# Front in one schedule: input in pieces, latent units by chunk, mask as contraction rows, attentions interleaved, output projection in halves

## The reference, cut to what matters

```python
n = rms_norm(h, attn_norm)
z = n @ w_in                     # gq, gk, gv, g_low, g_r, c_q, c_kv, k_r
# gated linear attention, 4 heads, chunks of 64
log_a = log_sigmoid(g_low @ gla_gate_w2 + gla_gate_b) / 16
o_g = rms_norm(gla_chunked(gq * 64 ** -0.5, gk, gv, log_a), gla_out_norm) * silu(g_r)
# latent attention, 8 heads of 96 (64 plain, 32 rotated)
q_m = rms_norm(c_q, mla_q_norm) @ mla_w_uq
k_nope, v_m = rms_norm(c_kv, mla_kv_norm) @ mla_w_ukv
q_m, k_m = rope(rms_norm(q_m, qk_norm_q)), rope(rms_norm([k_nope, k_r], qk_norm_k))
o_m = softmax(q_m @ k_m.T / sqrt(96), masked by chunk of 64) @ v_m
h = h + concat(o_g, o_m) @ w_out
h = h + square(relu(rms_norm(h, mlp_norm) @ w_mlp_up)) @ w_mlp_down    # and so on, not touched
```

## Time and profile before

| | |
|---|---|
| median of three timed runs | 1779.61 us (1776.09 to 1781.24) |
| profiled execution | 1769.77 us, span 1768.0 us |
| mean granted TensorE clock | 0.981 |
| busy | TensorE 97%, VectorE 55%, ScalarE 34%, GpSimd 8% |
| chain that ended last | TensorE 86%, VectorE 9%, ScalarE 2%, DMA 2% |
| loads of a 1 MB unit | 125, 4.8 us to landing |

### The profile page before, as it was taken

How to read it: one execution, slowest core, us unless ns; L and a number is a source line. 1 busy time by engine, 2 the same in 40 slices (tenths; PEclk the granted TensorE clock), 3 DMA queues, 4 the chain that set the end, 5 groups by cost and what they waited for, 6 DMA issues and landing times.

```text
span 1768.0 us, 19415 instructions
## 1 busy us (share of the span) xinstructions
PE 1713.6 (97%) x8226; PEld 1375.6 (78%) x8226; DVE 970.9 (55%) x1407; ACT 598.4 (34%) x832; POOL 149.8 (8%) x107
## 2 busy tenths in 40 slices
PE   5898999999999999999999999999999999999999
PEld 3776667878888888887888888887776888888887
DVE  5576654544434346675755645754647567456453
ACT  2243432432323133342322322344556433222211
POOL 2151000200000000240000000041100200000000
PEclk9997979999999999999999999999999999999999
DMA  4211000333333242221232222322212123222221
GB/s 173 96 66 54 1 1 1 108 90 140 90 116 102 104 122 97 72 72 63 104 119 96 95 97 77 128 79 101 76 60 95 48 95 113 102 96 95 96 77 66
DMA packets 27016, 154.00 MB, mean 87 GB/s; under 512 B 4657, under 2 KB 5825, under 8 KB 10929
## 3 DMA queue, kind: packets, MB, share of 16 engines
q1 hardware_dynamic: 24048, 147.62, 23.4%
q0 software_dynamic: 2592, 4.41, 1.7%
q10 hardware_dynamic: 288, 0.73, 0.1%
HBM read 148.01 MB, written 4.72 MB: 86 GB/s over the span
## 4 chain that ended last, share of the span: by engine, by line
PE 86%; DVE 9%; ACT 2%; DMA 2%; issue 1%; POOL 1%; SPq 0%; DVEq 0%; ACTq 0%; POOLq 0%
PE bank L519 22%; PE bank L521 22%; PE bank L520 22%; PE bank L525 3%; PE bank L527 3%; PE bank L526 3%; DVE WL L1513 2%; DMA RAW<-in_W 2%; PE bank L688 1%; PE bank L1087 1%; PE bank L1109 1%; PE bank L1096 1%; PE bank L715 1%; ACT WH L1153 1%; PE bank L689 1%; PE bank L728 1%
## 5 line engine op out<-in xcount | busy, mean ns | idle before, releaser
L519 PE MATMUL bank<-AH,WH 128*128 128x512 f32 (+1 forms) x1184 | 469.4, 396 | 21.1 <-DVE AL L1537 16.2
L521 PE MATMUL bank<-AH,WL 128*128 128x512 f32 (+1 forms) x1184 | 464.8, 393 | 0.0
L520 PE MATMUL bank<-AL,WH 128*128 128x512 f32 (+1 forms) x1184 | 464.3, 392 | 0.0
L1513 DVE TENSOR_TENSOR WL<-RAW,WH 128x2048 fp32r<-128x2048 f32 (+2 forms) x137 | 307.4, 2246 | 214.8 <-ACT WH L1153 214.8
L1153 ACT ACTIVATE WH<-RAW 128x2048 fp32r<-128x2048 f32 (+2 forms) x137 | 254.0, 1857 | 304.1 <-PE bank L521 258.8
L519 PEld LDWEIGHTS bank<-AH,WH 128*128 128x128 f32 (+1 forms) x1184 | 223.7, 189 | 74.8 <-issue 14.5
L520 PEld LDWEIGHTS bank<-AL,WH 128*128 128x128 f32 (+1 forms) x1184 | 223.9, 189 | 48.0 <-issue 2.1
L521 PEld LDWEIGHTS bank<-AH,WL 128*128 128x128 f32 (+1 forms) x1184 | 223.5, 189 | 48.2 <-issue 1.4
L519 PE MATMUL bank<-HH,WH 128*128 128x512 f32 x608 | 239.6, 394 | 0.0
L521 PE MATMUL bank<-HH,WL 128*128 128x512 f32 x608 | 238.4, 392 | 0.0
L520 PE MATMUL bank<-HL,WH 128*128 128x512 f32 x608 | 236.0, 388 | 0.0
(11 more groups left out here) (273 smaller groups left out, 1807.7 us busy)
## 6 DMA issues: line engine op xcount, KB each, us to landing
RAW<-in_W SPq DMA_DIRECT2D x125, 1024.0 KB, 4.8
RAW<-in_W SPq DMA_DIRECT2D x9, 768.0 KB, 4.3
ev_scratch<-ev POOLq DMA_DIRECT2D x4, 640.0 KB, 29.0
X<-in_XT SPq DMA_DIRECT2D x4, 512.0 KB, 10.5
Gb<-ev_scratch SPq DMA_DIRECT2D x16, 128.0 KB, 2.9
out<-X SPq DMA_DIRECT2D x8, 256.0 KB, 2.0
Gb<-ev_scratch SPq DMA_DIRECT2D x16, 112.0 KB, 2.6
RAW<-in_W SPq DMA_DIRECT2D x2, 512.0 KB, 6.2
```

What stands on the lines that cost most here:

```text
L519: e.matmul(o, a, h, start=first, stop=False)
L520: e.matmul(o, a, l, start=False, stop=False)
L521: return e.matmul(o, c, h, start=False, stop=last)
L1513: e.tensor_tensor(k.WL[u % NW][:, 0:n], k.RAW[u % NR][:, 0:n], k.WH[u % NW][:, 0:n].bitcast(F), SUB).then_inc(*WLO.mark(u))
```

## The change

- Input: eight pieces of one tile, on two queues; ScalarE makes `AH`, VectorE only `AL` and the additions of the squares, GpSimd none. The constants are loaded after the input.
- Latent units by chunk: `small` and `ckv` become one unit of 192 columns (`lkv`); it and `cq` are multiplied channel tile by channel tile as `AL` comes. `norm_spread` follows both. `gq` goes between the column sums. Six banks rotate instead of four.
- Heads: `qm` and `km` hold heads outside and 100 instead of 96 columns; columns 96 to 99 hold, per block of 128 tokens, a one (query, first chunk) or -1e30 (key, second chunk), so the score product masks itself. Gains go into the copy of the transposed head (plain part) and into the rotation's tables; the query's root goes into the exponential's scale, one root of 32 columns per side instead of four of 8.
- Steps: one head transpose per step, ahead of use, all copied by ScalarE, into four query and four key buffers; the maximum is taken by an operation that also copies the scores out; the weights are scaled by VectorE and turned by a transpose.
- Output projection: units by half of the channels. `attended` takes the attention's half for all eight output tiles, between the linear attention's last stages; the other half follows as two more units. `X` gets two additions per tile. `AT` lies in the `RAW` buffer that the first MLP unit loads into, so that load waits for the last low part `ol`. The MLP's norm takes tiles 4 to 7 first.

```diff
-        for x in range(4):
-            a, l = split_view(k, wu[x // 2], 8)
...
+    for c in range(4):
+        low_and_values(c)
+    for c in range(4):
+        low_queries(c)
+    for c in range(4, 8):
+        low_and_values(c)
+        low_queries(c)
...
-                e.matmul(bank[b][:, 0:n], k.qT[hh][0:MQ, q * P:(q + 1) * P], k.kT[hh][0:MQ, 0:n], start=True, stop=True)
-                e.matmul(bank[b][:, n - P:n], cst[0:1, C_MA:C_MA + P], cst[0:1, C_MB:C_MB + P], start=False, stop=True,
-                         skip_group_check=True).then_inc(*MM.mark("s1", i, hh))
+                e.matmul(bank[hh][:, 0:n], k.qT[y][0:MK, q * P:(q + 1) * P], k.kT[y][0:MK, 0:n], start=True, stop=True).then_inc(
+                    *MM.mark("s1", i, hh))
...
-                    t = e.matmul(bank[4 + hh][:, c * P:(c + 1) * P], pb[2 * (u % 3) + hh][:, c * P:(c + 1) * P], dg[:, x, :],
-                                 start=True, stop=True, skip_group_check=True)
+                    t = e.transpose(bank[4 + hh][:, c * P:(c + 1) * P], pb[2 * (u % 3) + hh][:, c * P:(c + 1) * P], ident)
...
+        if i < 3 * NT:
+            head(q % 2, 2 * p + 2 + q // 2, 2)
...
+    attended(0)
+    attended(1)
+    outputs(0)
+    attended(2)
+    outputs(1)
+    attended(3)
+    out_sums(0)
+    out_sums(1)
+    attended(4)
+    out_sums(2)
+    out_sums(3)
+    attended(5)
+    spread_out(0)
+    attended(6)
+    spread_out(1)
+    attended(7)
+    spread_out(2)
+    spread_out(3)
...
# scalar_program
+    fill(4)
+    split(6)
     for q in range(NT):
-        fill(1)
         w.wait_ge(MM("ukv", q, 1), POOL("rq3"))
         e.activation(k.vm[:, q, :], bank[k.where["ukv", q, 1]][:, :], AF.Copy, scale=k.rq3[:, 4 + q:5 + q]).then_inc(*ACT.mark("vm", q))
...
# sync_program
+        if u == UNIT["up", 0]:
+            w.wait_ge(DVE("ol", 3))
```

More of the change, by code:

```diff
@@ L480, in fill_order @@
 def fill_order():
[L482 to L492, removed]
+    out = [("squares", 0, q) for q in range(NT)]
+    out += [("root", 0, 0), ("angles", 0, 0), ("tables", 0, 0), ("turn1", 0, 0), ("turn2", 0, 0)]
+    out += [("squares", 1, q) for q in range(NT)]
+    out += [("root", 1, 0), ("tables", 1, 0), ("turn1", 1, 0), ("turn2", 1, 0)]
+    return out + [("norm", 1, q) for q in range(NT)]
 def mla_steps():
@@ L673, in tensor_program, with head @@
     ptb = k.t2s + sq
+    def head(x, g, b):
+        w.wait_ge(DVE("norm1", 3) if x else DVE("rope", 0), POOL("seen"), *free[b])
+        for c in range(NT):
+            t = e.transpose(bank[b][0:MK, c * P:(c + 1) * P], (k.qm, k.km)[x][:, g, c, :], ident)
+        t.then_inc(*in_bank(b, "head", x, g))
+        free[b] = [ACT("head", x, g)]
+    for n, (x, g) in enumerate(((0, 0), (0, 1), (1, 0), (1, 1))):
+        head(x, g, (2, 4, 5, 6)[n])
     for i, p, q in mla_steps():
-        if p < MH // 2:
+        if i < 4 * NT:
@@ L862, in low_of @@
+    MM.also("unit", u)
+    u = UNIT["wout", 3]
+    a, l = split_view(k, u, 4)
+    w.wait_ge(WLO(u))
+    for x in range(4):
+        cols = slice(x * P, x * P + P)
+        b = (6, 7, 4, 5)[x]
+        w.wait_ge(*free[b])
+        for c in range(4):
+            t = triple(bank[b][:, :], a[:, c, cols], l[:, c, cols], AH[:, c, :], AL[:, c, :], c == 0, c == 3)
+        t.then_inc(*in_bank(b, "res", 16, x))
+        free[b] = [DVE("x", 16, x)]
+    MM.also("unit", u)
+    ring[0] = 0
     def low_of(n):
@@ L1558, in vector_program, with scaled_query @@
             *DVE.mark("cl", i))
+    def scaled_query(i):
+        w.wait_ge(MM("gq", i))
+        e.scalar_tensor_tensor(k.gq[:, i, :], bank[where["gq", i]][:, :], GK ** -0.5, rb[:, :], MUL, MUL).then_inc(*DVE.mark("gq", i))
+    low_rank(0)
+    low_rank(1)
+    low_rank(2)
+    split(3)
+    scaled_query(0)
+    w.wait_ge(MM("small"))
+    e.tensor_tensor(k.low[:, :], bank[where["small",]][0:64, :], rb[0:64, :], MUL).then_inc(*DVE.mark("low"))
     w.wait_ge(MM("csum", 2))
@@ L1663, in vector_program @@
             fill(2)
-    for half in range(2):
-        split(11 + half)
-        for q in range(NT):
-            fill(1)
-            if half:
-                w.wait_ge(MM("gv", 1, q))
-                e.tensor_scalar(k.gv[:, q, :], bank[where["gv", 1, q]][:, :], k.r4[:, q:q + 1], None, MUL).then_inc(*DVE.mark("gv", q))
-    fill(21)
+    fill(21)
+    split(10)
+    split(11)
+    for q in range(NT):
+        w.wait_ge(MM("gv", 1, q))
+        e.tensor_scalar(k.gv[:, q, :], bank[where["gv", 1, q]][:, :], k.r4[:, q:q + 1], None, MUL).then_inc(*DVE.mark("gv", q))
     for j in range(2):
@@ L1793, in vector_program, with attended @@
             t.then_inc(*DVE.mark("state", j, c))
+    def attended(m):
+        add_to_x(1, m, bank[where["res", 1, m]][:, :], MM("res", 1, m))
+    for m in range(4):
+        attended(m)
+    split(UNIT["wout", 2], MM("og", 3))
     w.wait_ge(MM("osum", 3))
     e.tensor_scalar(k.mg[:, :], bank[7][:, 0:16], 1.0 / GV, EPS, MUL, ADD).then_inc(*DVE.mark("mg"))
+    attended(4)
+    split(UNIT["wout", 3])
     def out_diagonal(h):
```

714 lines of the change are left out of this document (337 added, 377 removed).

## The result

The changed kernel takes 1729.58 us (median of four runs, 1728.55 to 1731.42) against 1780.42 for the kernel before in the same comparison (four runs, 1776.09 to 1781.27): ratio 0.972, 95% interval 0.9702 to 0.9739. Timed again beside the experiments it takes 1729.15 against 1775.01, ratio 0.9757 (0.9718 to 0.9796). The forecast was 1727.6, from 1714 to 1752. The time is right to 2 us, but not for the reasons given: the profiled spans are 1768.0 and 1728.0 us, 40.0 apart, where the sum of the steps said 52. Twelve microseconds were over-estimated, and an offset that did not hold covered them.

What follows compares the result with a forecast made beforehand. TensorE, busy for 97% of the span, was taken as the bound. Projections -22, attention -33 and output projection +3 gave -52 us: 1717.8 us as profiled, 1727.6 as median with the 9.8 us offset, range 1714 to 1752.

Steps and rivals of the forecast that it cites:

- Projections: Stage from 0 to 153 us in the kernel before: to end at 131 us, a gain of 22 us.
- the stall: Key-value product: TensorE waits 4.4 us from 64.6 us for ScalarE's copy of v, then 2 us of low level.
- Attention: Stage from 153 to 276 us in the kernel before: to take 90 us, a gain of 33 us.
- the allowance for waits: Attention: 10% of waits on top of 70.9 us of TensorE work, making 80 us at full clock.
- Output projection: Stage from 276 to 338 us in the kernel before: to take 65.2 us, 3 us more (0 to 8).
- the MLP's gap: First MLP unit: VectorE's low part of block 0 comes 2.9 us late, then 1 us of low level.
- The offset: Whole kernel: profiled execution 9.8 us under the median of timed runs, expected to stay after the change.
- A: Attention: no half clock, the forecast without its 10 us, 1717.6 us; chance 0.22.
- B: Attention: two half-clock stretches as before, 1737.6 us; chance 0.19.
- C: Attention: half clock throughout the stage, 157 us with waits, 1795 us in all; chance 0.08.
- D: Attention: interleaving doesn't mesh, steps stay about 5.5 us, 1750 us in all; chance 0.12.
- E: Whole kernel: time moves from the front to waits of the same size, within 5 us of before; chance 0.04.

Runs made afterwards that it cites:

- e1_ukv: Changed kernel with ScalarE's copies of v moved ahead of the third and fourth squaring and the weight split: 1721.19 us.
- e6_pool: Changed kernel with GpSimd again adding the squares in the input stage and VectorE making only low parts: 1729.18 us.
- e2_keep_ol: Changed kernel with VectorE's masked copy ahead of scaling and maximum, and a pair's low part taken at the next step's head: 1715.46 us.
- e4_mask: Changed kernel with a one-row product that adds nothing put back after each of the 32 score products: 1752.42 us.
- e3_tail: Changed kernel with VectorE's last wout low part after the first diagonal and the first MLP unit loaded into the other input buffer: 1721.67 us.
- e9_before_look: Kernel before, unaltered, profiled once more: 1779.32 us; another such profile took 1769.84 us.
- e7_best: Changed kernel with the edits of e1_ukv, e2_keep_ol and e3_tail plus two more, in the last attention steps and the output projection: 1690.91 us.
- after_again: Changed kernel, unaltered, timed once more beside the kernel before: 1729.15 us.

## Why the prediction was right and where it was wrong

**Projections: right.** TensorE started at 11.47 us (11.9 said), gq at 38.10 (37.8), the stall stood at 69.87 and lasted 4.40 us, ended by ScalarE's copy of v (69.0 and 4.4), the first scores came 20.9 us earlier (22). Mis-sized: the slow matmuls after the stall, 2 us said and 4.2 by e1_ukv; gv ended at 131.1, not 128.0. The transposes ahead of the scores gained 4.5 us instead of 2.4. One reason given for the start is not borne out: GpSimd's additions, put back beside the later half of the input, cost nothing (e6_pool).

**Attention: right in kind, 7 us too good.** The stage was to be 70.9 us of work, 9.1 of waits and 10 us of half clock, 90 us. Measured to the same point (229 us, 3 us behind the first state product) it is 98: by the estimate above 67.4 us of work, 17.5 idle and 13.0 lost to the clock. The step that failed is the allowance for waits, 17.4 us instead of 9.1. It was a share taken over from the kernel before at full clock (5.6 of 58 us), when the text of the change shows the cause: `keep` was the first thing in VectorE's step before, and TensorE waited for it 1.80 us at the turn of a pair all the same; in after it stands behind scaling, two maxima and, once per pair, a wait for ScalarE. e2_keep_ol put it first and got 13.7 us back. The half clock cost 3 us more than forecast and came in another form: not one stretch of 20 us, but three of 7 to 9 us, each behind a wait of 3 or 4 us, and a shorter one at 140 us behind a wait of 1.70 us. The work fell by more than was booked (90.1 to 64.6 us, 25.5 instead of 22.3): e4_mask makes the mask products 18.2 us instead of 13.1, since each also lengthened the score product ahead of it.

**Output projection: sign right, 7 us too small.** First spread 3.58 us instead of 1.5, because VectorE's weight split ahead of it waited 2.70 us for ScalarE's high part and started only at 257.29; the MLP's gap was as forecast (2.71 against 2.9 us). The term mis-sized beside it is the low clock: 4.2 us are lost between 226 and 318 us where 1 was allowed, most of it behind the 3.58 us; before, nothing was lost there. e3_tail gave 7.5 of the 10.0 us back.

**Behind the front: 3 us of gain, forecast as nothing.** A wait of 3.73 us for a weight split became 2.05.

**The offset: wrong.** "I expect that offset to stay" took one execution's distance from three others for a property of the program. A difference of that size is one half-clock stretch more or less in the kernel before (e9_before_look). The errors of the sum (+1.1, +6.9, +7.0, -3.0 by the table: 12.0 us) and the missing offset (9.8 us) cancelled, by luck: the first comparison, which gives a gain of 50.8 us, had only executions of the last two lines of the table for the kernel before; against the median of the 33 later executions, 1774.2, the gain is 45 us, and the sum's 52 is 7 too many.

**Rivals.** A fell (there was half clock) and so did B (13.0 us were lost to it, not 20). C fell: the clock came back each time, and e7_best holds 1.00 for 66 us with all transposes in it. The rule of the Trainium skill behind C (TensorE: Matmul & The Clock Gate, section "Part 4: PE-mode transpose", that the full clock does not engage for transposes) does not show for transposes mixed with other products as here; a stream of transposes alone no run had. D gave 105 us for the stage plus 8 for a stretch; measured 98 with them, and in e7_best eight steps at the full clock took 33.0 us (score products of 152.08 and 185.06 us), 4.1 each, against 5.5 by D and 4.7 forecast. E fell.

## What to carry over

When an engine's work is reordered, list for every bank or buffer who frees it and what now stands ahead of that operation in its engine's order; the operation that frees goes first, the one that waits for another engine goes last or a step later. In these runs waits of TensorE cost about twice their length (4.4 us of wait 8.6, 6.4 us 13.5), and where TensorE is busy but slow, look for the gap ahead of the stretch. Before adding an offset between a profile and timed runs, compare their mean granted clocks: they may be executions from different steps of the same ladder.

## What the runs showed of the hardware

- The same program ran in four groups of times, 1761 to 1782 us. Profiles of two of them, 9.5 us apart, differ by 20 us more or less at half clock in the attention (e9_before_look against the trace of before). The same waits are not always followed by the same clock: with TensorE busy for 7.55 or 7.56 us of 131 to 141 us in all three, after shows a clock of 0.83 in 141 to 147 us, after_again 0.91 and e3_tail 0.50.
- During such a stretch TensorE is busy to 100%, and the granted clock does not rise for that: 20.00 of 20.00 us at 0.51, 19.70 of 20 at 0.58 in e4_mask.
- 32 columns of GpSimd's power take 5.43 us in after, 16 took 2.90, 8 take 1.65 and 4 take 1.04 us.
- A product of one row with 127 columns added 0.56 us to a score product, 0.41 between its start and the next one's and 0.15 on the product ahead of it (e4_mask against after).
